# Expert loop of a two-block transformer kernel: the one weight half that was multiplied whole is split as well, and POOL makes its low part

## The reference, cut to what matters

```python
def expert_block(args):
    xb, e = args
    hgu = xb @ w_up_gate[e] + b_up_gate[e]            # 128x1024 @ 1024x2048
    x_glu = jnp.minimum(hgu[:, :D_EXPERT], SWIGLU_LIMIT)
    x_lin = jnp.clip(hgu[:, D_EXPERT:], -SWIGLU_LIMIT, SWIGLU_LIMIT)
    hact = x_glu * jax.nn.sigmoid(SWIGLU_ALPHA * x_glu) * (x_lin + 1.0)
    return hact @ w_down[e] + b_down[e]                # 128x1024 @ 1024x1024
```

## Time and profile before

| | us |
|---|---|
| median of 3 runs | 2566.66 (2564.89 to 2574.68) |
| the profiled execution, its own time | 2565.02 |
| span of that execution in the profile | 2563.2 |
| PE busy | 2368.1 (92% of the span) |
| DVE busy | 1780.3 (69%) |
| ACT busy | 1334.2 (52%) |
| POOL busy | 149.5 (6%) |

### The profile page before, as it was taken

How to read it: one execution, slowest core, us unless ns; L and a number is a source line. 1 busy time by engine, 2 the same in 40 slices (tenths; PEclk the granted TensorE clock), 3 DMA queues, 4 the chain that set the end, 5 groups by cost and what they waited for, 6 DMA issues and landing times.

```text
span 2563.2 us, 31147 instructions
## 1 busy us (share of the span) xinstructions
PE 2368.1 (92%) x10716; PEld 1867.0 (73%) x10716; DVE 1780.3 (69%) x2142; ACT 1334.2 (52%) x1520; POOL 149.5 (6%) x103
## 2 busy tenths in 40 slices
PE   5999988999998998677799999999999999999967
PEld 4865566888787885555577777877777787777756
DVE  7526645555624667564688888889888888988863
ACT  4353343333413236204467766776776677677643
POOL 1000000000000000001001110110111011011100
PEclk8989898999999999777799999999999999999998
DMA  8213303332121310216799999999999999999960
GB/s 312 87 66 106 141 1 99 99 99 95 41 78 66 113 66 1 91 48 230 256 357 368 360 361 369 365 361 366 367 361 362 367 365 357 370 368 360 364 227 33
DMA packets 286442, 570.40 MB, mean 223 GB/s; under 512 B 10500, under 2 KB 34983, under 8 KB 286343
## 3 DMA queue, kind: packets, MB, share of 16 engines
q1 hardware_dynamic: 273607, 523.69, 56.6%
q0 software_dynamic: 12768, 45.81, 6.5%
HBM read 542.70 MB, written 26.75 MB: 222 GB/s over the span
## 4 chain that ended last, share of the span: by engine, by line
PE 85%; DVE 7%; ACT 3%; issue 2%; DMA 1%; SPq 1%; DVEq 0%; POOL 0%; ACTq 0%; POOLq 0%
PE bank L1633 13%; PE bank L1635 13%; PE bank L1634 13%; PE bank L1303 6%; PE bank L1305 6%; PE bank L1304 6%; PE bank L1627 4%; PE bank L1284 4%; PE bank L1492 3%; PE bank L1493 3%; PE bank L1494 3%; PE bank L1622 2%; PE bank L1381 2%; PE bank L1363 1%; PE bank L1609 1%
## 5 line engine op out<-in xcount | busy, mean ns | idle before, releaser
L2211 DVE TENSOR_TENSOR w_lo<-stage,w_hi 128x2048 fp32r<-128x2048 f32 x364 | 818.6, 2285 | 73.2 <-ACT w_hi L1200 72.6
L1200 ACT ACTIVATE w_hi<-stage 128x2048 fp32r<-128x2048 f32 x364 | 685.5, 1912 | 228.2 <-PE bank L1635 223.9
L1633 PE MATMUL bank<-w_hi,xeT_hi 128*128 128x512 f32 x1056 | 439.3, 416 | 0.0
L1635 PE MATMUL bank<-w_hi,xeT_lo 128*128 128x512 f32 x1056 | 412.9, 391 | 0.0
L1634 PE MATMUL bank<-w_lo,xeT_hi 128*128 128x512 f32 x1056 | 412.6, 391 | 0.0
L1635 PEld LDWEIGHTS bank<-w_hi,xeT_lo 128*128 128x128 f32 x1056 | 199.0, 188 | 43.0
L1634 PEld LDWEIGHTS bank<-w_lo,xeT_hi 128*128 128x128 f32 x1056 | 199.7, 189 | 40.4
L1633 PEld LDWEIGHTS bank<-w_hi,xeT_hi 128*128 128x128 f32 x1056 | 200.5, 190 | 37.2
L1760 DVE TENSOR_TENSOR ring_low<-ring,half_top 128x2048 fp32r<-128x2048 f32 (+2 forms) x42 | 93.1, 2221 | 161.9 <-ACT half_top L943 161.6
L1305 PE MATMUL bank<-half_top,hT_low 128*128 128x512 f32 (+1 forms) x480 | 188.7, 393 | 0.0
L1633 PE MATMUL bank<-w_hi,eaT_hi 128*128 128x512 f32 x400 | 176.0, 440 | 0.0
(11 more groups left out here) (414 smaller groups left out, 3860.3 us busy)
## 6 DMA issues: line engine op xcount, KB each, us to landing
stage<-in_w_up_gate SPq DMA_DIRECT2D x264, 1024.0 KB, 7.5
stage<-in_w_down SPq DMA_DIRECT2D x132, 1024.0 KB, 5.1
ring<-in_w_ada SPq DMA_DIRECT2D x12, 2048.0 KB, 8.2
ring<-in_w_up SPq DMA_DIRECT2D x22, 1024.0 KB, 7.7
ring<-in_w_in SPq DMA_DIRECT2D x10, 2048.0 KB, 7.8
ring<-in_w_out SPq DMA_DIRECT2D x4, 2048.0 KB, 13.2
ring<-in_w_down SPq DMA_DIRECT2D x4, 2048.0 KB, 8.0
stage<-in_w_ple_gate SPq DMA_DIRECT2D x4, 1024.0 KB, 7.2
```

The source lines that it names most:

```text
L1200: fn(w_hi[top_of(h)][:, :], src[:, :], ACT.Copy).then_inc(s_hi, 1)
L1633: mm(bank[b][:, :], hi[:, kk, :], wh[:, k, :], start=False, stop=False)
L1635: ins = mm(bank[b][:, :], lo[:, kk, :], wh[:, k, :], start=False, stop=kk == KT - 1)
L2211: tt(w_lo[h][:, :], stage[h][:, :], w_hi[top_of(h)][:, :].bitcast(FP), ALU.subtract).then_inc(s_lo, 1)
```

## The change

Half 8 is treated as the other eleven: ACT makes its high part (`split_hi(i, 8, 9)`), and `fill` multiplies it with three fp32r matmuls for each block. Its low part is made by POOL, in the loop ahead of its gather; PE waits for it on a semaphore of its own. The buffer `ea_whole` and ACT's copy into it go. With twelve split halves the rotation over six high buffers comes out the same in each iteration, so that some high parts stand in another buffer than before. DVE's instructions stay what they were.

```diff
-WHOLE = 8
-SPLIT = [h for h in range(HALVES) if h != WHOLE]
+SPLIT = list(range(HALVES))
+BY_POOL = 8
+BY_DVE = [h for h in SPLIT if h != BY_POOL]
...
             with pool.Fori(1, nb) as i:
+                h = BY_POOL
+                pool.wait_ge(s_hi, split_no(i, h))
+                nc.gpsimd.tensor_tensor(w_lo[h][:, :], stage[h][:, :], w_hi[top_of(h)][:, :].bitcast(FP), ALU.subtract).then_inc(s_lo_pool, 1)
                 pool.wait_ge(s_idx, i + 2)
                 pool.wait_ge(bank_full[6], 2 * i + FU[6])
                 pool.wait_ge(bank_full[7], 3 * i + (FU[7] + 2))
...
-            def tiles_T(dst, k6, k7, whole=None):
+            def tiles_T(dst, k6, k7):
...
-                    if j == 0 and whole is not None:
-                        fn(whole[:, :, :], blk3(bank[b][:, :]), ACT.Copy)
                     fn(dst[0][:, 4 * j:4 * j + 4, :], blk3(bank[b][:, :]), ACT.Copy).then_inc(s_xhi, 1)
...
-                tiles_T(eaT, 2 * i + (FU[6] + 1), 3 * i + (FU[7] + 3), ea_whole)
-                split_hi(i, 9)
+                tiles_T(eaT, 2 * i + (FU[6] + 1), 3 * i + (FU[7] + 3))
+                split_hi(i, 8, 9)
...
                 for h in (h0, h0 + 1):
-                    if whole is not None and h == WHOLE:
-                        wv = half_in(pe, i, h)[:, :].rearrange("p (k n) -> p k n", k=KT // 2)
-                        for k in range(KT // 2):
-                            ins = mm(bank[b][:, :], whole[:, k, :], wv[:, k, :], start=False, stop=False)
+                    if h == BY_POOL:
+                        pe.wait_ge(s_lo_pool, i)
                     else:
-                        pe.wait_ge(s_lo, split_no(i, h))
+                        pe.wait_ge(s_lo, low_no(i, h))
+                    wh, wl = (a[:, :].rearrange("p (k n) -> p k n", k=KT // 2) for a in (w_hi[top_of(h)], w_lo[h]))
+                    for k in range(KT // 2):
+                        kk = h % 2 * (KT // 2) + k
+                        mm(bank[b][:, :], hi[:, kk, :], wh[:, k, :], start=False, stop=False)
+                        mm(bank[b][:, :], hi[:, kk, :], wl[:, k, :], start=False, stop=False)
+                        ins = mm(bank[b][:, :], lo[:, kk, :], wh[:, k, :], start=False, stop=kk == KT - 1)
```

More of the change, by code:

```diff
@@ L42 @@
 BEHIND = len([h for h in SPLIT if h >= 8])
+BEHIND_V = len([h for h in BY_DVE if h >= 8])
 S_MAX = 0.9999933123588562
@@ L239, in program @@
     ey = at(R + 64 * KB, [P, D], name="ey")
-    ea_whole = at(R + 68 * KB, [P, KT // 2, P], name="ea_whole")
     el = [at(R + (72 + 2 * i) * KB, [P, CW], name=f"el{i}") for i in range(2)]
@@ L511, in program @@
     stage_in = [sem(f"stage_in{h}") for h in range(HALVES)]
-    s_hi, s_lo = sem("half_hi"), sem("half_lo")
+    s_hi, s_lo, s_lo_pool = sem("half_hi"), sem("half_lo"), sem("half_lo_pool")
     half_read = [sem(f"half_read{h}") for h in range(0, HALVES, 2)]
@@ L631, in split_no, with low_no @@
         return n + 1 + BEHIND if isinstance(i, int) and i == 0 else i * len(SPLIT) + (n + 1)
+    def low_no(i, h):
+        n = BY_DVE.index(h)
+        return n + 1 + BEHIND_V if isinstance(i, int) and i == 0 else i * len(BY_DVE) + (n + 1)
     def half_in(eng, i, h):
@@ L1617, in turn, with fill @@
                     ins.then_inc(bank_full[b], 1)
-            def fill(b, lhs, hot_, bcol, i, h0, whole=None):
+            def fill(b, lhs, hot_, bcol, i, h0):
                 hi, lo = lhs
@@ L1623, in fill @@
                 for h in (h0, h0 + 1):
-                    if whole is not None and h == WHOLE:
-                        wv = half_in(pe, i, h)[:, :].rearrange("p (k n) -> p k n", k=KT // 2)
-                        for k in range(KT // 2):
-                            ins = mm(bank[b][:, :], whole[:, k, :], wv[:, k, :], start=False, stop=False)
-                    else:
-                        pe.wait_ge(s_lo, split_no(i, h))
[L1630 to L1635, removed]
+                    if h == BY_POOL:
+                        pe.wait_ge(s_lo_pool, i)
+                    else:
+                        pe.wait_ge(s_lo, low_no(i, h))
[5 more added lines that the diff above has]
+                        ins = mm(bank[b][:, :], lo[:, kk, :], wh[:, k, :], start=False, stop=kk == KT - 1)
                     ins.then_inc(half_read[h // 2] if h == h0 else bank_full[b], 1)
@@ L1646, in up, with down @@
                 fill(c, xeT, hot[0], c * CW, i, 2 * j)
-            def down(i, at_, h0, k6, k7, whole):
+            def down(i, at_, h0, k6, k7):
                 pe.wait_ge(bank_taken[6], k6)
@@ L1654, in down @@
                     pe.wait_ge(bank_taken[4 + n], TK[4 + n] + i)
-                    fill(4 + n, eaT, hot[1], 2 * D + n * CW, at_, h0 + 2 * n, whole)
+                    fill(4 + n, eaT, hot[1], 2 * D + n * CW, at_, h0 + 2 * n)
             def turn_ea(i, k6, k7):
@@ L1683, in _ @@
                 turn(rows, 2 * i + (TK[6] + 1), 3 * i + (TK[7] + 4))
-                down(i - 1, i, 8, 2 * i + (TK[6] + 1), 3 * i + (TK[7] + 3), ea_whole)
+                down(i - 1, i, 8, 2 * i + (TK[6] + 1), 3 * i + (TK[7] + 3))
             turn_ea(nb - 1, 2 * nb + TK[6], 3 * nb + (TK[7] + 2))
-            down(nb - 1, nb, 0, 2 * nb + (TK[6] + 1), 3 * nb + (TK[7] + 3), None)
+            down(nb - 1, nb, 0, 2 * nb + (TK[6] + 1), 3 * nb + (TK[7] + 3))
             norm(4)
@@ L1704, in _ @@
             ve = nc.vector
-            dve.nop().then_inc(s_lo, BEHIND)
+            dve.nop().then_inc(s_lo, BEHIND_V)
             tt, ts, stt = ve.tensor_tensor, ve.tensor_scalar, ve.scalar_tensor_tensor
```

## The result

| | us | to before, 95% interval |
|---|---|---|
| before, median of the 4 runs beside it | 2567.99 | 1 |
| changed kernel, median of 4 | 2818.11 (2808.48 to 2827.6) | 1.0968 [1.0936, 1.1000] |
| its profiled execution: own time, span | 2815.94, 2814.0 | |

The change costs 9.7%, 250 us, where 1.1% was forecast, and lies far outside the range. Mean granted TensorE clock is 0.911, against 0.950.

A forecast was written before the change was run, and what follows sets the result against it. PE was taken as the bound, at 37.43 us an iteration. A saving of 0.72 and a 1.7 us wait for the gather gave +0.98, times 32 +31 us, so 2596 us, 1.1% slower; range 2540 to 2630.

The forecast's parts named there:

- What the change saves, 0.72 us an iteration: PE's first down product falls from 6.42 to 5.70 us, saving at most 23.0 us over 32 iterations.
- ACT costs nothing: ACT's added high part of 1.92 us was costed at nothing, covered by its 29% free time.
- POOL's own price of 4.6 us: POOL's subtraction of 128x2048, taken as the middle of bounds 3.8 and 5.5 us.
- So POOL starts when the low part of half 6 ends: POOL, ready during DVE's low part of half 6, waits only for that instruction, starting at 1619.80, done at 1624.4.
- rival 3: POOL is held off by low parts 6, 7 and 9; PE waits 6.1 us; +5.4 an iteration, 2737 us; chance 0.08.
- The landing of 7.3 us: Gather's time from issue to landing, from one earlier gather; rows land 1.7 us after PE's transposes want them.
- its step of 0.16 for 0.30: On POOL, the gather was forecast to follow the subtraction's end by a step of 0.30 us.
- A wait of PE costs its length: PE's new wait for the gather, before its transposes, was added to the iteration as 1.7 us.
- DVE is 0.7 us short of being the bound: DVE, if kept out 4.6 us, ends its hot row at 1643.55; PE wants it at 1644.3.
- Rival 2: POOL runs ahead of DVE's low part of half 6, DVE becomes the bound; +0.4 us an iteration, 2577 us; chance 0.2.

The follow-up runs named there:

- pe_only: dve12 with half 8's low part left out, PE multiplying its high part twice instead; 2543.17 us, 0.9904 of the kernel before.
- dve12_found: dve12 with DVE's copy `picked` and row numbers moved ahead of the gated unit and half 10's low part; 2548.18 us, 0.9921 of the kernel before.
- late_release: Changed kernel with DVE waiting for ACT's high part of half 9 between its low parts of 6 and 7; 2666.17 us, 1.0379 of the kernel before.
- gather_first: Changed kernel with POOL's subtraction moved behind its gather; 2647.08 us, 1.0311 of the kernel before.
- dve_yields: Changed kernel with DVE waiting for POOL's subtraction before its low part of half 6; 2677.69 us, 1.0432 of the kernel before.
- dve12: Changed kernel with DVE making all twelve low parts, half 8's included, and POOL none; 2578.87 us, 1.0047 of the kernel before.
- pool_memset: Changed kernel with POOL writing zeros in place of the subtraction, leaving out half 8's low part; 2613.27 us, 1.0176 of the kernel before.
- pool_repaired: Changed kernel with the subtraction behind the gather, DVE waiting for it before half 6, and the copy `picked` earlier; 2607.09 us, 1.0151 of the kernel before.

## Why the prediction was wrong

Its steps, in its own order:

- **What the change saves, 0.72 us an iteration: right.** pe_only and dve12_found have 0.73.
- **ACT costs nothing: right.** POOL was ready 0.07 us behind the high part. DVE's low parts started 0.17 us ahead of POOL, also as forecast.
- **POOL's own price of 4.6 us: right.** 4.62 undisturbed, about 4.8 where it had waited.
- **"So POOL starts when the low part of half 6 ends": the step that failed.** It starts when the low part of half 9 ends, 6.51 us behind the moment when it is ready, where the forecast had 2.1. That a waiting POOL instruction gets the next boundary between two low parts was taken from one kind of instruction at one place, the gather between the low parts of 4 and 5. The case that happened is rival 3, which had the chance 0.08 and 2737 us. The evidence for its low chance was that single pattern, seen 31 times in 34 gathers (2.13 to 2.26 us) but always at the same place of the iteration. late_release, where POOL does get in behind half 6 in 20 of 32 iterations, runs in 2666 us. That is still 70 us above the forecast, so with this step right 2596 would probably still have been too low: the next points are in that run too.
- **The landing of 7.3 us: near.** It is 7.9. With POOL's 4.8 for 4.6 and its step of 0.16 for 0.30, PE's wait becomes 6.6 us, where rival 3's sum has 6.1.
- **A wait of PE costs its length: the second step, and a tacit one.** It costs 1.94 us more, in the transposes and the first down product at the lower clock. 32 times this is 62 us of the 251, and it is most of the distance from rival 3's 2737 to the 2818 measured; the rest is that 0.5 us of longer wait.
- **"DVE is 0.7 us short of being the bound": a link was missing.** DVE was followed only to its hot row. Its copy `picked` is wanted earlier, by the second four of PE's transposes. In the changed kernel the late gather hides this; wherever the gather comes in time (gather_first, dve_yields, dve12) it is what PE waits for next. Rival 2, POOL in front of the low part of half 6, is what dve_yields makes: 2678 us, and not 2577. Also missing was that POOL, once in, holds DVE's `glu` for 4.3 us.

The sum mended by what the rows of after show, in the iteration shown for PE: POOL is ready at 1596.01, waits 6.51, works 4.80, and issues the gather 0.16 later, at 1607.48; the rows are there at 1615.40, 7.9 later; PE is ready at 1615.40 - 6.59 = 1608.81. So -0.72 + 6.59 + 1.94 = +7.8 us, as measured.

**Left open:** why a gather gets in between two low parts that follow each other (2.24 us in the earlier trace rows; 2.86 in late_release), while the gather of pool_memset, the subtraction and every scatter that met such a run were held to its end. The length of the run alone does not tell: the gathers that got in stood in the first of two low parts, but one scatter of pool_repaired (at 2501.86 us), which also came in the first of two, was held through both (5.07 us). And in dve_yields the gather starts 0.03 us behind a low part and is not held at all (0.98 us, in 31 iterations). No run here separates the kinds.

## What to carry to other kernels

Count a POOL subtraction of two SBUF inputs beside two-input DVE work as one that starts when DVE's whole unbroken run ends, not its current instruction. An indirect DMA may be held as long (each scatter here was, and the gather of pool_memset) or get in earlier (the gathers of the kernel before), so give it both bounds. Then add DVE's own wait behind it. Put spare work on POOL only if nothing with a deadline stands behind it in its queue, and if DVE can spare the time: with the gather out of the way and everything mended, POOL's 4.6 us kept DVE from its work for longer than the 2.2 us that it saved it. Here the work was cheaper on an engine at 86%, which took it at no cost once one early copy had been moved. And price a new wait of PE at more than its length, since the clock may be down when it ends.

## What the runs showed that was not expected

- A run of low parts also holds POOL's scatter (7.25 us against 1.6, dve12; 9.47 in pool_repaired), and in pool_memset the gather (5.66 against 0.98). In dve12_found the scatter takes 7.0 to 8.4 us in 30 of 33 cases, and nothing waits for it.
- The clock fell to 0.57 in a wait of 6.6 us, and was down in dve_yields too (0.72 in the 4 us from 1624) behind a wait of 2.33 us; in gather_first, whose waits are as long (2.3 us at the longest), it is 0.99 in the mean of 2000 to 2367 us, in dve_yields 0.96. What makes the difference between these two is not shown.
